# A chain of two transformer blocks: two differential heads, the product P times V and some squares change engine or place

## What is computed

```python
q, k, v, z, xbc, dt_raw, gate_logits = jnp.split(h @ w_in, cuts, axis=-1)
# differential attention, 8 heads of 128 values, causal
p = softmax(q1 k1) - lam * softmax(q2 k2);  o = p v
o = _rmsnorm(o, da_subln_g, SUBLN_EPS) * (1.0 - lam_init)
attn_out = o.reshape(b, s, DA_V) @ w_branch_attn
# state-space branch
yg = (y * jax.nn.silu(z)).reshape(b, s, SSD_GROUPS, SSD_INNER // SSD_GROUPS)
y = _rmsnorm(yg, ssd_norm_g, SUBLN_EPS)
ssd_out = y.reshape(b, s, SSD_INNER) @ w_branch_ssd
g_attn, g_ssd = jnp.split(jax.nn.sigmoid(gate_logits + b_gate), N_BRANCH, axis=-1)
mixed = (g_attn * attn_out + g_ssd * ssd_out) @ w_mix_out
```

```python
h = jnp.sin(freq_1 * (z @ w_f1 + b_f1))             # filter network, two such layers
q = rms_norm(q, g_qn); k = rms_norm(k, g_kn)        # each head, 96 wide, k_rope shared
attn = softmax(rotary(q) rotary(k)^T / sqrt(96)) v  # v: 64 a head, not causal
u_attn = (attn * jax.nn.silu(z_attn)) @ w_attn_out
x = x + (g_hy * u_hy + g_at * u_attn) @ w_out
```

## Time and profile before

| | us |
|---|---|
| median of 3 runs | 1203.13 |
| lowest and highest of them | 1202.48 to 1203.32 |
| the profiled execution | 1203.46 |
| its span in the profile | 1201.7 |
| PE busy | 1160.4 |
| DVE busy | 773.6 |
| ACT busy | 571.2 |

### The profile page before, as it was taken

How to read it: one execution, slowest core, us unless ns; L and a number is a source line. 1 busy time by engine, 2 the same in 40 slices (tenths; PEclk the granted TensorE clock), 3 DMA queues, 4 the chain that set the end, 5 groups by cost and what they waited for, 6 DMA issues and landing times.

```text
span 1201.7 us, 20882 instructions
## 1 busy us (share of the span) xinstructions
PE 1160.4 (97%) x8518; PEld 1074.0 (89%) x8518; DVE 773.6 (64%) x1072; ACT 571.2 (48%) x809; POOL 0.2 (0%) x4
## 2 busy tenths in 40 slices
PE   8999999999999999987999999999999999899998
PEld 6999999999999999977988797999999599888888
DVE  6645446768888867876566747454454656975654
ACT  5443345567653345746335445433433446444352
POOL 0000000000000000000000000000000000000000
PEclk9999999999999999997999999999999999999999
DMA  8655554554543353442455244355555435342241
GB/s 318 221 187 193 175 193 156 203 183 155 185 140 110 118 190 141 141 141 103 172 166 193 89 140 158 133 183 176 191 192 176 140 133 184 133 149 95 82 141 36
DMA packets 28526, 189.60 MB, mean 158 GB/s; under 512 B 3400, under 2 KB 4713, under 8 KB 6378
## 3 DMA queue, kind: packets, MB, share of 16 engines
q1 hardware_dynamic: 25984, 181.41, 43.5%
q10 hardware_dynamic: 2474, 7.20, 1.8%
HBM read 187.55 MB, written 1.05 MB: 157 GB/s over the span
## 4 chain that ended last, share of the span: by engine, by line
PE 76%; DVE 16%; ACT 5%; issue 2%; DMA 1%; DVEq 0%; SPq 0%; ACTq 0%
PE bank L445 22%; PE bank L447 22%; PE bank L446 22%; DVE sb_w_lo L1723 4%; PE bank L510 2%; ACT sb_w_hi L1124 2%; DVE sb_ssd_conv L1893 1%; PE bank L677 1%; PE bank L1011 1%; PE bank L999 1%; DMA sb_w_raw<-in_w 1%; PE bank L1055 1%; PE bank L1033 1%; ACT sb_da_p L1368 1%; PE bank L897 0%
## 5 line engine op out<-in xcount | busy, mean ns | idle before, releaser
L1723 DVE TENSOR_TENSOR sb_w_lo<-sb_w_raw,sb_w_hi 128x2048 fp32r<-128x2048 f32 x171 | 391.2, 2290 | 199.9 <-ACT sb_w_hi L1124 196.1
L445 PE MATMUL bank<-sb_hT_hi,sb_w_hi 128*128 128x256 f32 x1576 | 450.2, 286 | 6.5 <-DVE sb_w_lo L1723 5.2
L446 PE MATMUL bank<-sb_hT_lo,sb_w_hi 128*128 128x256 f32 x1576 | 443.7, 282 | 0.0
L447 PE MATMUL bank<-sb_hT_hi,sb_w_lo 128*128 128x256 f32 x1576 | 443.4, 281 | 0.0
L1124 ACT ACTIVATE sb_w_hi<-sb_w_raw 128x2048 fp32r<-128x2048 f32 x171 | 326.6, 1911 | 99.2 <-PE bank L447 97.6
L445 PEld LDWEIGHTS bank<-sb_hT_hi,sb_w_hi 128*128 128x128 f32 x1576 | 297.2, 189 | 11.2 <-DVE sb_w_lo L1723 7.4
L446 PEld LDWEIGHTS bank<-sb_hT_lo,sb_w_hi 128*128 128x128 f32 x1576 | 297.4, 189 | 2.4 <-issue 1.2
L447 PEld LDWEIGHTS bank<-sb_hT_hi,sb_w_lo 128*128 128x128 f32 x1576 | 297.3, 189 | 0.1
L445 PE MATMUL bank<-sb_w_hi,sb_hT_hi 128*128 128x256 f32 (+1 forms) x304 | 87.3, 287 | 1.9 <-DVE sb_w_lo L1723 0.8
L446 PE MATMUL bank<-sb_w_lo,sb_hT_hi 128*128 128x256 f32 (+1 forms) x304 | 84.9, 279 | 0.0
L1172 ACT ACTIVATE sb_ffn_gate<-bank 128x256 f32<-128x256 f32 x44 | 16.9, 385 | 142.7 <-PE bank L447 142.7
(11 more groups left out here) (384 smaller groups left out, 1683.7 us busy)
## 6 DMA issues: line engine op xcount, KB each, us to landing
sb_w_raw<-in_w SPq DMA_DIRECT2D x171, 1024.0 KB, 5.0
sb_x<-in_x SPq DMA_DIRECT2D x1, 1024.0 KB, 5.4
sb_mem_xn<-in_mem ACTq DMA_DIRECT2D x1, 1024.0 KB, 7.1
sb_post_g<-in_ffn_post_g ACTq DMA_DIRECT2D x2, 512.0 KB, 4.1
sb_dft_f<-in_c_dft ACTq DMA_DIRECT2D x1, 1024.0 KB, 7.0
out<-sb_x SPq DMA_DIRECT2D x4, 256.0 KB, 2.2
sb_post_g<-in_mix_post_g ACTq DMA_DIRECT2D x1, 512.0 KB, 5.3
sb_w_f<-in_w_f ACTq DMA_DIRECT2D x1, 512.0 KB, 5.0
```

Source lines behind the costliest of these rows:

```text
L445: pe.matmul(o, a_hi, b_hi, start=first, stop=False)
L446: pe.matmul(o, a_hi, b_lo, start=False, stop=False)
L447: return pe.matmul(o, a_lo, b_hi, start=False, stop=last)
L1723: tt(w_lo[b % STAGES][:], w_raw[b % RING][:], f32(w_hi[b % STAGES][:]), ALU.subtract).then_inc(w_lo_in, 1)
```

## The change

It has four parts, in four places of the program:
1. In the z and gate loop the bias of the gates goes from DVE to ACT; DVE takes the maxima of a head, then splits the weights, then makes the probabilities; y times silu(z) is at the end of i = 9, the squares on ACT at i = 10 and 11, the scaling of y at the start of i = 11. Only heads 0 to 5 are worked through here. Heads 6 and 7 are in `ssd_out`: scores after its blocks 0 and 1, turns after 2 and 3, P times v after 3 and 4. Scaling of the heads' outputs comes on DVE after the split of block 4, their turn after block 6. The turns of y use other banks; three of them are made inside the first block of `ssd_out`. The gated product is written into the gate's own buffer.
2. In `attn_out` the rounding and the split of the next weights come before the copies of the sum; argument and sine of the first filter layer come after the last block.
3. The squares of the latent q and k are taken on ACT (128 x 1536); for q, 1/root goes into the scale of the exponential in place of a product; the parts of the head norm stand among the short convolutions; the copy of k_rope is earlier.
4. P is turned without having been divided by its sum. P times V has the turned P as weights and 64 columns of V as the moving part, so the result is token-major; DVE scales it by 1/sum (`at_scale`), PE turns a pair of heads (`at_turn`, two transposes), DVE multiplies by silu(z_attn) (`at_gate`). The last pair's turn stands between the two halves of the second block of `hy_out`. The sigmoid of the gates is earlier in ACT's list.

The diff, cut to its core:

```diff
@@ PE, z and gate loop, ssd_out @@
-                o = claim(f"yT{kp}", (3, 7, 4, 3, 7, 7, 7, 4)[kp])
+                o = claim(f"yT{kp}", (5, 6, 3, 4, 7, 5, 6, 7)[kp])
...
-                if i % 2 == 0:
-                    if i:
-                        da_turn(i // 2 - 1)
+                if 2 <= i <= 12 and i % 2 == 0:
+                    da_turn(i // 2 - 1)
+                if i <= 10 and i % 2 == 0:
                     da_scores(i // 2)
-                elif i > 1:
+                if 3 <= i <= 13 and i % 2:
                     da_out(i // 2 - 1)
-            da_turn(DA_HEADS - 1)
             y_turn(7)
             y_turn(0)
-            y_turn(1)
-            da_out(DA_HEADS - 1)
-            y_turn(2)
-            y_turn(3)
...
+                    if i == 0 and n in (2, 4, 6):
+                        y_turn(n // 2)
...
                 ssd_block(i)
-                if i == 4:
+                if i in (3, 4):
+                    da_out(i + 3)
+                if i in (2, 3):
+                    da_turn(i + 4)
+                if i in (0, 1):
+                    da_scores(i + 6)
+                if i == 6:
                     pe.wait_ge(S("da_on"), 2)
@@ PE, latent heads @@
-                pe.wait_ge(S("m_P"), 2 * h + 2)
+                wait_read(pe, f"ms{h}")
...
-                    mm = pe.matmul(banks[5][r, 0:SEQ], mv[:, kb, h, :], m_PT[:, kb, :], start=kb == 0, stop=kb == 1)
+                for q in range(2):
+                    at = q * P + h % 2 * V_DIM
+                    for kb in range(2):
+                        mm = pe.matmul(banks[5][:, at:at + V_DIM], m_PT[:, kb, q * P:(q + 1) * P], mv[:, kb, h, :],
+                                       start=kb == 0, stop=kb == 1)
@@ ACT, z and gate loop, attn_out, second block @@
+                if i >= 8:
+                    gate_bias(i - 8)
...
             for i, c in enumerate(MIXED):
+                if i < 3:
+                    after(FIRST["attn_out"] + i)
                 act.wait_ge(S("mixed"), i + 1)
                 act.activation(mixed_hi[:, c, :], mg[:, c, :], ACT.Copy).then_inc(S("mixed_hi"), 1)
-                if i < 3:
-                    after(FIRST["attn_out"] + i)
-                if i == 2:
-                    hidden_sin(0)
             after(FIRST["attn_out"] + 3)
+            hidden_sin(0)
...
+            act.activation(msq[:], mq[:, 0], ACT.Square).then_inc(S("msq_in"), 1)
             after(FIRST["uq"] + 1)
@@ DVE, z and gate loop @@
+                if i <= 10 and i % 2 == 0:
+                    da_max(i // 2)
+                if i < 15:
+                    low_after(FIRST["z"] + i)
+                if i <= 10 and i % 2 == 0:
+                    da_probs(i // 2)
@@ DVE, second block @@
-            head_norm(0)
-            head_turn(0)
+            head_sums(0)
+            link(ts(m_rs[:], rstd[:], QK_DIM ** -0.5, None, ALU.mult))
+            head_gain(0)
+            low_after(FIRST["ukv"])
+            centred_conv(0)
+            low_after(FIRST["hy"])
+            head_turn(0)
...
+                if i in (4, 6, 8):
+                    at_gate(c)
+                if i in (3, 5, 7):
+                    at_scale(c)
```

More of the change, by code:

```diff
@@ L1052, in mla_out, with at_turn, wide_out @@
                     claim(f"mo{h // 2}", 5)
-                r = slice(h % 2 * V_DIM, (h % 2 + 1) * V_DIM)
-                for kb in range(2):
-                    mm = pe.matmul(banks[5][r, 0:SEQ], mv[:, kb, h, :], m_PT[:, kb, :], start=kb == 0, stop=kb == 1)
+                for q in range(2):
[3 more added lines that the diff above has]
+                                       start=kb == 0, stop=kb == 1)
                 if h % 2:
                     ends(mm, f"mo{h // 2}")
-            def wide_out(key, b, hi, lo, at, ready=None):
+            def at_turn(c, bank):
+                wait_read(pe, f"mo{c}")
+                o = claim(f"aT{c}", bank)
+                for t in range(TOK):
+                    mm = turn(o[:, t * P:(t + 1) * P], at_tok[:, t].rearrange("p h d -> p (h d)"))
+                ends(mm, f"aT{c}")
+            def wide_out(key, b, hi, lo, at, ready=None, between=None):
                 feature_block(f"{key}.0", b, 2, hi, lo, HY_TILES, 512, bank=at[0], last=False, ready=ready)
+                if between:
+                    between()
                 feature_block(f"{key}.1", b, 2, hi, lo, HY_TILES, 512, bank=at[1], at=256)
@@ L1608, in _ @@
                 copy(f"uq1.{t}.0", mq_rows[:, 0, t, 512:768], o[:, 0:256])
+            for t in range(TOK):
+                wait_read(act, f"uq0.{t}.0")
+                wait_read(act, f"uq1.{t}.0")
+            act.activation(msq[:], mq[:, 0], ACT.Square).then_inc(S("msq_in"), 1)
             after(FIRST["uq"] + 1)
@@ L1616, in _ @@
             after(FIRST["ukv"])
+            for t in range(TOK):
+                for h in (0, 512):
+                    wait_read(act, f"ukv.{t}.{h}")
+            act.wait_ge(S("k_rope_in"), 1)
+            act.wait_ge(S("msq_read"), 1)
+            act.activation(msq[:], mq[:, 1], ACT.Square).then_inc(S("msq_in"), 1)
             def centre_tap(i):
@@ L1665, in _ @@
                     read(ins, f"gg{i}")
+                if i >= 8:
+                    for j in range(8):
+                        wait_read(act, f"gg{j}")
+                    c = slice(8 * (i - 8), 8 * (i - 7))
+                    act.activation(gate2[:, c, :], gate2[:, c, :], ACT.Sigmoid).then_inc(S("gate2"), 1)
                 if i == 0:
@@ L1685, in _ @@
                 after(FIRST["gate2"] + i)
-                if i >= 8:
-                    for j in range(8):
-                        wait_read(act, f"gg{j}")
-                    c = slice(8 * (i - 8), 8 * (i - 7))
-                    act.activation(gate2[:, c, :], gate2[:, c, :], ACT.Sigmoid).then_inc(S("gate2"), 1)
             for i in range(4):
@@ L2043, in da_probs @@
                         .then_inc(S("da_P"), 1)
-            def gate_bias(i):
-                o = full(dve, f"gate{i}")
-                for c in range(2):
-                    ins = ts(mix_gate[:, 2 * i + c, :], o[:, c * SEQ:(c + 1) * SEQ], col("b_gate", 2 * i + c), None, ALU.add)
-                read(ins, f"gate{i}")
             def y_low(kp):
```

194 lines of the change are left out of this document (114 added, 80 removed).

## The result

The changed kernel takes 1174.45 us (median of four executions, 1174.06 to 1175.48), against 1203.22 before (now the median of four as well): a ratio of 0.9763, with a 95% interval from 0.9746 to 0.978. The forecast was 1175.6. The profiled execution took 1174.42 with a span of 1172.6, which is 29.1 less than the span before.

A forecast was written before the change was run, and what follows sets the result against it. PE was taken as the bound, so only its idle time and lower clock could pay. Terms -18.9 - 2.7 - 7.0 + 1.1 = -27.5 from 1203.46 give 1175.9, stated as 1175.6; range 1169 to 1185.

The forecast's parts named there:

- Gate blocks and projection, -18.9: Gate blocks and first projection block: 19.4 us lost to idle and low clock goes, 0.5 returns; bounds -19.4 and -14.
- about 16 us leave a DVE queue: Gate blocks: two moved heads take 12.4 us and four more gate biases 3.5 off DVE, where PE idled 13.4.
- The 0.5 for a bank in the first block: First projection block: PE waits for DVE's y6 before a turn of y gets its bank, 0.5 us, bounds 0 and 2.3.
- The heads' new place, 0: State-space projection: two heads moved in cost PE nothing, as DVE and ACT have room; 0 to 8 us as rival.
- A: Projection or attn_out: moved heads bring their waits along, 3 to 8 us, about 1181; chance 0.12.
- D: Projection: waits of some 3 us ahead of four blocks lower the clock, 23 us, slower than before; chance 0.03.
- E: Gate blocks: the gain comes in part, -14 in place of -18.9, with waits for banks, 1180.5; chance 0.08.
- Attn_out and mix_out, -2.7: End of attn_out, start of mix_out: the 2.78 us wait and low clock go, part returns; bounds -4.3 and 0.
- Head norm, -7.0: Hyena columns: 5.2 us off DVE and splits between norm parts recover 7.0 of 7.1 us; bounds -7.1 and -2.
- rival B: Hyena columns stay bound by DVE as key squares come late from ACT; 5 of 7.1 us remain, 1180.6; chance 0.10.
- Latent heads, +1.1: Latent heads: P times V gives -1.3 us, eight transposes add 0.9, the last pair's turn waits 1.5.
- rival C: Latent heads: narrow P times V costs by columns, 0.50 us a head, -4.1 over eight, about 1172.8; chance 0.05.

The follow-up runs named there:

- the four edits: Undone together in the changed kernel (heads 6 and 7 back, gate bias on DVE, probabilities ahead of the split, scaling of y behind it): 1185.85 us.
- The two experiments: Changed kernel with both latent-head squares back on DVE: 1175.94 us; changed kernel with head norms each in one piece in their old places: 1177.07 us.
- the version with further edits: Changed kernel with splits moved behind norm-row scaling, last pair's scaling and hy_out's second gate ahead of splits, gate bias on DVE: 1167.02 us.

## Why the prediction was right, step by step

**What bounds the kernel.** Right: only PE's idle time and its clock counted. The three stretches that the windows named (19.4, 4.3 and 7.1 lost) gave 18.97, 2.9 with the stretch behind it, and 7.53. By the medians the change gave 28.8 where the sum was 27.5; the latent heads' term is off by as much (+1.1 against -0.18).

**Gate blocks and projection, -18.9.** The sum is right to 0.1, its parts are not. The step "about 16 us leave a DVE queue" gave 12.4 to the two heads and 3.5 to the bias as if they were terms that add. They do not add: the heads give 6.56 when they are the only edit, but undone alone they cost 0.98, so that the other three keep 10.72 of the 11.70 without them; the bias gives 4.62 alone, and undone alone it costs nothing. (That 6.56 and 4.62 come near to 11.70 doesn't make them terms.) And the step lacked the last split's place, with the 4.56 us that PE waited for it: some 7.3 of the 19 lie outside the four edits. I had read the whole loss of the stretch off the window and let it go with the idle; that holds because all of the loss went, not because of the terms that I gave. The time in hand was right: the scaled y was ready 2.9 us ahead of its turn, where I had 2.8:

```profile
511.14 3.26 DVE L2120 TENSOR_SCALAR sb_ssd_y<-sb_ssd_y,sb_rstd 128x512 f32<-128x512 f32 x8
517.35 0.60 PE L514 MATMUL bank<-sb_square,sb_ssd_y 128*128 128x128 f32 x4
```

The scaling begins at 511.14 and ends at 514.40, and the turn at 517.35 has no wait in its row. The 0.5 for a bank in the first block was 0.55 (the idle time in the window from 511.3).

**The heads' new place, 0.** Right, and with it rivals A, D and E fall: no wait of PE is left in the projection's window. The tight step was as tight as forecast: the low half of o is ready at 584.66, 0.36 ahead of attn_out's start at 585.02, where I had 0.4:

```profile
581.94 2.72 DVE L2170 SCALAR_TENSOR_TENSOR sb_o_lo<-bank,sb_sub_g,sb_o_hi 128x512 fp32r<-128x512 f32 x4
```

**Attn_out and mix_out, -2.7.** Measured -2.9 from the start of attn_out to the products behind the turns. But the terms are again uneven: undone, it cost 1.34 in the traces and 1.7 in the medians, since there the clock did not fall. The table load was not on the chain at all, as these rows of ACT show:

```profile
612.78 1.28 ACT L1500 ACT_TABLE_LOAD   x1
617.88 0.42 ACT L1500 ACTIVATE sb_hid<-sb_hid 64x256 f32<-64x256 f32 x1 [3.81 <-DVE sb_hid L2188]
```

The load (1.28) was over 3.81 us before the argument was there. The 0.9 that I let the chain give back was 1.38 to 1.46 (2.8 to 4.2 in the wait for the rows), and the 0.7 for the longer idle time was 0.22, in the turns behind it.

**Head norm, -7.0.** Measured -7.53, 0.4 beyond the bound of 7.1. The two experiments give 1.79 to the squares and 2.84 to the order; the 2.9 left were not run apart. That DVE stays under PE held, but narrowly: it is busy for 35.25 of the 36.60 us of the columns. No wait for weights is left there, so rival B falls.

**Latent heads, +1.1.** This is the term that was mis-sized: -0.18. The product took 0.84 a head as forecast, and rival C falls (its 0.50):

```profile
1053.48 1.00 PE L1063 MATMUL bank<-sb_mv,sb_m_PT 128*128 128x64 f32 x8
1054.32 0.61 PE L514 MATMUL bank<-sb_square,sb_m_p 128*128 128x128 f32 x4
```

But a head gained more than its product: from one gate block to the next, with the same work otherwise, it was 9.12 us before (1091.99 to 1101.11) and 8.80 after (1062.35 to 1071.15), 0.32 less, of which 0.17 are the product's own and 0.09 are a gap ahead of it that is gone. Seven heads at that rate are 2.2, and the last one, which has other work around it, gained 0.1 (1155.65 to 1156.65 before, 1124.85 to 1125.76 after): 2.3 instead of 1.3. The wait of the last turn was 0.99, not 1.5, and with the 0.9 for the turns the terms come to -0.4:

```profile
1129.83 0.44 PE L514 MATMUL bank<-sb_square,sb_at_tok 128*128 128x128 f32 x2 [0.99 <-DVE sb_at_tok L2423]
```

## What to carry to other kernels

Read the loss of a stretch from its window (length less count times the full-rate price) before pricing single edits: the sum was right because the loss was, and edits that shorten one queue do not add, so that undoing them one by one shows little; take all of them away as well, and put them back one by one. Look for a shared engine's item that waits for another engine and has the bottleneck's next operand queued behind it, as the last weight split did here (by the traces; it was not run alone); moving it adds no work. Where PE waits for a norm, take everything out of that chain that the next product doesn't need.

## What the runs showed that I had not expected

The same idle time of PE, 2.78 us ahead of the same product, was followed by a granted clock of 0.72 over 6 us in one kernel and of 1.00 in another, so the clock's price of an idle time of this length isn't a fixed term. And shortening an idle time need not pay in every execution. In the profiled one of the version with further edits the wait ahead of cross attention is 2.16 shorter, but the first 96 products behind it took 13.85 us, against 11.62 in the changed kernel (up to 12.79 in others with the same wait of 4.2). From the start of these products to the next norm's turn it is 75.10 against 75.07, although the wait ahead of that turn is shorter too, 0.64 in place of 2.84. The windows from the turn on, first in that version, then in the changed kernel:

```profile
644.00:647.00 3.00, 2.40 (x17) 2.03 (x16) 3.00 (x5) 2.56 (x8) 0.00 (x0) 0.68 0.00 0
647.00:651.00 4.00, 4.00 (x19) 4.00 (x20) 4.00 (x7) 0.47 (x2) 0.00 (x0) 0.50 0.78 266
651.00:656.00 5.00, 5.00 (x41) 5.00 (x40) 3.71 (x4) 0.96 (x2) 0.00 (x0) 0.91 0.00 0
656.00:661.00 5.00, 5.00 (x43) 4.95 (x42) 2.29 (x1) 1.72 (x2) 0.00 (x0) 1.00 0.08 11
```

```profile
646.00:650.00 4.00, 3.37 (x17) 3.37 (x17) 1.92 (x5) 2.18 (x6) 0.00 (x0) 0.50 0.08 35
650.00:655.00 5.00, 5.00 (x44) 5.00 (x43) 5.00 (x7) 1.11 (x3) 0.00 (x0) 1.00 0.01 3
655.00:661.50 6.50, 6.50 (x57) 6.50 (x56) 5.00 (x4) 2.40 (x2) 0.00 (x0) 1.00 0.00 0
```

The half clock (0.50, the lower of the two levels, 1.2 GHz) came in both. In the changed kernel it fell on the 16 turns, which took 3.60 us where the 16 at 577.52 took 1.91; with the shorter wait the turns ran faster (2.48) and the half clock fell on the products behind them. But this was one execution: the windows above lose 3.4 us of clock, which is all that its mean granted clock of 0.997 leaves room for, while three of the other four executions of that version had a mean of 0.999 or 1.0 and took 1166.46 to 1167.02. So little low clock fits into those that the shorter wait must have paid there for the most part, and the median shows it.
